# A causal depthwise convolution shared out anew between TensorE, VectorE, ScalarE and GpSimd, and another order of attention groups, in a two-layer encoder

## Chip, cores and metric

One core of one Trainium2 chip runs the whole kernel. The metric is the device time in microseconds of one execution, as the median of several runs.

## The reference

Input `x` is 1 x 256 x 1024 float32. Two layers, each a mixer and a feed-forward part, all with a residual sum. What bears on the change is the convolution module of layer 0 and the attention of layer 1:

```python
def conformer_conv_module(h, ...):
    u = h @ pw1_w + pw1_b
    a, gate = jnp.split(u, 2, axis=-1)
    u = a * jax.nn.sigmoid(gate)
    u = lax.conv_general_dilated(u, dw_w[:, None, :], window_strides=(1,),
        padding=[(CONV_WIDTH - 1, 0)], feature_group_count=D_MODEL, ...) + dw_b
    u = jax.nn.silu(layernorm(u, ln_g, ln_b))
    return u @ pw2_w + pw2_b
```

CONV_WIDTH is 31 and each of the 1024 channels has its own 31 taps. The layer norm is over the channels, so it needs all of them. Layer 0 then has a dense SwiGLU of width 2816. Keys and values for 4 heads are computed once from its result. Layer 1 is attention with 16 query heads of 64, four to a key head, over the own and the previous chunk of 64 tokens, with a learned sink per head and a relative-position bias:

```python
    scores = jnp.where(valid, scores + bias, -1e30)
    m = jnp.maximum(jnp.max(scores, axis=-1, keepdims=True), s)
    p = jnp.exp(scores - m)
    probs = p / (jnp.sum(p, axis=-1, keepdims=True) + jnp.exp(s - m))
    out = jnp.einsum("bckgqj,bcjkd->bcqkgd", probs, v_band)
    return out.reshape(B, S, N_HEADS * HEAD_DIM) @ w_o
```

A top-2-of-8 expert SwiGLU of width 3584 and a final norm end the kernel.

## The kernel before

The kernel is written engine by engine. Each engine has a fixed program, and semaphores join them; the order of work is the order in which it is written. PE is TensorE, DVE VectorE, ACT ScalarE, POOL GpSimd, SP the engine that issues most transfers.

Weights come in units of 1 MB through a ring of seven slots, issued by SP (L398, L453). From the dense stage on, a weight is used as the sum of two float32r parts: ACT copies a half unit (`high_parts`, L666), DVE subtracts the copy from the original (`low_parts`, L1410), and PE makes three passes (`three_passes`, L974). There is room for four halves of parts. A slot of the ring is loaded anew once DVE has split both of its halves (`split_done`). A `column_product` makes two 128-column pieces of a transposed product, a `row_product` adds one unit to the output in token rows.

**The convolution.** The 1024 channels are eight chunks of 128, a channel to a partition. The first pointwise product (L915) makes value and gate of two chunks at a time, on PE. ACT takes the sigmoid of a gate (L615), two buffers deep, and DVE multiplies (`glu`, L1349) into `upad`, which holds the chunk with 30 columns of zeros ahead. Then two engines share the 31 taps. DVE does chunks 0 to 4, one instruction of 128 x 256 a tap (`conv_tap`, L1356 for the first tap, L1359 for the others): each adds a shifted input times the tap's weights to the chunk, so a tap of a chunk waits for the one before it. Chunks go in pairs, (0,1), (2,3), and 4 alone; a further `glu` comes after every sixteen taps. PE does chunks 5 to 7: for a tap, one matmul (two records in the trace) of the shifted chunk with a diagonal matrix of the tap's weights, added up in a PSUM bank (L938). The diagonals are identity times the tap's column. ACT makes those with even numbers (L633), POOL those with odd ones (L517), into a ring `taps` of four that lies in `R1`, where the input of the first product is too; so they begin when that product is done, and each waits until the one four before it is used. ACT evicts a finished chunk with its bias (`conv_out`, L622). PE sums the chunks' columns with a matrix of 1/1024 (`add_to_mean`, L925): chunks 0 to 3, 5 and 6 ahead of the last four taps, 4 and 7 after them. DVE subtracts the mean (L1391), and the variance, the scaling and the second product (L961) follow.

**Attention.** Four groups, one for each key head. The unit of the query weights of a group is `U_Q + g`, that of the output weights `U_O + g`. For a group: `query_product` on PE, `queries` on ACT (copy with a scale), `scores` on PE (L1093) into two banks, `softmax_front` on DVE (sum with the bias, L1500; maximum, L1504; its negative with the sink, L1507), `exps` on ACT (L728), `softmax_sum` on DVE (L1514, L1515), the multiplication with the reciprocal on POOL (L559), `values` on PE (transposes L1102, ACT's copies `probs_T` L737, the product with V L1111) and `heads_out` on DVE (L1523, L1525), and `out_product` (L974). Groups of one parity share a pair of banks, a half of `prob` and a half of `bias`, so `scores(g)` waits for `heads_out(g - 2)`, and `softmax_front(g)` for the transposes of g - 2. POOL loads the bias of groups 0 and 1 ahead of the stage. Its program in the stage is, for g = 0 to 3: wait for the reciprocals, multiply, and for g = 0 and 1 issue the four transfers of the bias of group g + 2 (L544), wait for them and clear a corner (L549):

```python
                if g < 2:
                    pool.wait_ge(biased, 2 * g + 2)
                    load_bias(g + 2)
                    cut_bias(g + 2)
```

The experts follow with 336 units of weights, and take about two thirds of the time.

Of the kernel before, what the change touches and what calls it, by code (L numbers as in the profile page):

```python
# [57 lines left out]
DIAGS = 4  # L58
# [29 lines left out]
def expert_units():  # L88

    order = [("g", 0), ("u", 0)]  # L90
    for b in range(1, EB):
        order += [("g", b), ("u", b), ("d", b - 1)]
    order.append(("d", EB - 1))
    return [(kind, b, part) for kind, b in order for part in range(2)]


def trunk(nc, x, norm_mix_g, norm_ffn_g, conv_pw1_w, conv_pw1_b, conv_dw_w, conv_dw_b, conv_ln_g,
# [4 lines left out]
    with ctx:  # L102
# [62 lines left out]
        taps = R1[:, 1024:1024 + DIAGS * P].rearrange("p (b c) -> p b c", b=DIAGS)  # L165
# [85 lines left out]
        tap_pool = sem("tap_pool")  # L251
# [229 lines left out]
        def _(pool):  # L481
# [29 lines left out]
            product_done(pool, U_PW2 - 1)  # L511
            pool.wait_ge(cv_ready, 2)
            for m in range(1, PE_CHUNKS * CONV, 2):
                if m >= DIAGS:
                    pool.wait_ge(tap_used, m - DIAGS + 1)
                c, w = DVE_CHUNKS + m // CONV, m % CONV
                pool.tensor_scalar(taps[:, m % DIAGS, :], ident[:, :], dw[:, c, w:w + 1], 1.0, ALU.mult,  # L517
                                   ALU.mult).then_inc(tap_pool, 1)
# [58 lines left out]
        def _(sa):  # L577
# [39 lines left out]
            sa.wait_ge(cv_ready, 2)  # L617

            def conv_out(c):

                sa.wait_ge(tap_used, CONV * (c - DVE_CHUNKS + 1))
# [3 lines left out]
            conv_next = DVE_CHUNKS  # L625
            for m in range(0, PE_CHUNKS * CONV, 2):
                if m >= CONV * (conv_next - DVE_CHUNKS + 1) + DIAGS:
                    conv_out(conv_next)
                    conv_next += 1
                if m >= DIAGS:  # L630
                    sa.wait_ge(tap_used, m - DIAGS + 1)
                c, w = DVE_CHUNKS + m // CONV, m % CONV
                sa.mul(taps[:, m % DIAGS, :], ident[:, :], dw[:, c, w:w + 1]).then_inc(tap_act, 1)  # L633
            for c in range(conv_next, DC):
                conv_out(c)

# [109 lines left out]
            probs_T(0)  # L746
            exps(1)
            queries(3)
            high_parts(U_O + 1)
            probs_T(1)  # L750
            exps(2)
            high_parts(U_O + 2)
            probs_T(2)
            exps(3)
            high_parts(U_O + 3)
            probs_T(3)
# [101 lines left out]
        def _(pe):  # L858
# [59 lines left out]
            def add_to_mean(chunks):  # L918

                for c in chunks:  # L920
                    if c < DVE_CHUNKS:
# [7 lines left out]
            for m in range(PE_CHUNKS * CONV):  # L929

                c, w = DVE_CHUNKS + m // CONV, m % CONV
                if m % 2 == 0:
                    pe.wait_ge(tap_act, m // 2 + 1)
                else:
                    pe.wait_ge(tap_pool, m // 2 + 1)
                if w == 0:
                    pe.wait_ge(glu_ready, c + 1)
                mm = pe.matmul(PB[4 + m // CONV][:, 0:S], taps[:, m % DIAGS, :], upad[:, c, w:w + S],  # L938
                               start=(w == 0), stop=(w == CONV - 1))
                mm.then_inc(tap_used, 1)  # L940
                if m == PE_CHUNKS * CONV - 5:

                    add_to_mean([0, 1, 2, 3, 5, 6])
            add_to_mean([4, 7])
# [184 lines left out]
            scores(1)  # L1129
            values(0)  # L1130
            query_product(3)
            scores(2)
            values(1)
            out_product(0)
            scores(3)
            values(2)
            out_product(1)
# [150 lines left out]
        def _(ve):  # L1288
# [75 lines left out]
            pairs = [range(c, min(c + 2, DVE_CHUNKS)) for c in range(0, DVE_CHUNKS, 2)]  # L1364
            work = [(c, w) for pair in pairs for w in range(CONV) for c in pair]
# [4 lines left out]
            nxt = 2  # L1370
            for m, (c, w) in enumerate(work):
                if m % 16 == 15 and nxt < DC:
                    glu(nxt)
                    nxt += 1
                if w == 0:
                    ve.wait_ge(glu_ready, c + 1)
                else:
# [163 lines left out]
            softmax_sum(3)  # L1541
            low_parts(U_O + 3)
            heads_out(3)
# [231 lines left out]
```

## Time and profile before

| what | value |
|---|---|
| median of 3 runs | 1449.49 us (1448.54 to 1451.72) |
| the profiled execution | 1450.4 us, of which its span is 1448.7 us |
| PE, DVE, ACT, POOL busy | 98%, 81%, 68%, 4% of the span |
| mean granted clock of PE | 0.994 |

The profile is of one execution. Its page gives the busy time of each engine and the chain of work that ended last; the timelines give the instructions of an engine with start and duration in us, merged where they follow each other, and in brackets the idle time before them with what ended it. A busy PE means that a matmul is in flight, not that it is at its peak. Names are those of SBUF tensors: `R` stands for `R1`, `R2` and `R3`.

### The profile page before, as it was taken

The page shows a single profiled execution, that of the slowest core. Times are in us where ns is not written, and L with a number is a line of the kernel's source. Part 1 is how long each engine was busy: PE and PEld are TensorE (multiplying, and loading weights), DVE is VectorE, ACT ScalarE, POOL GpSimd, SP SyncE. Part 2 cuts the span into 40 slices and gives each one's busy share as a digit, 9 for nine tenths or more (in the row PEclk, how much of TensorE's full clock was granted, in tenths as well). Part 3 has the DMA queues.
Part 4 walks back from the last instruction along what each step waited for, and adds up shares of the span by engine and source line. Part 5 has one row for each costly group of instructions (what it writes and reads, how often), then busy time and mean ns, then how long its engine had stood idle before and what let it go on. Part 6 is the DMA issues. An engine that isn't in the chain of part 4 may idle for free.

```text
span 1448.7 us, 21504 instructions
## 1 busy us (share of the span) xinstructions
PE 1419.3 (98%) x7289; PEld 1193.2 (82%) x7289; DVE 1172.8 (81%) x1321; ACT 982.8 (68%) x1197; POOL 63.2 (4%) x108
## 2 busy tenths in 40 slices
PE   8999999999899999999999999999999999999997
PEld 8886899998878888888888888888888888888885
DVE  3793354456668998999999899899989989998996
ACT  2045343445646878877887877788888778877875
POOL 1060000002220000000000000000000000000000
PEclk9999999999999999999999999999999999999998
DMA  9500665555544999999899999999999999999991
GB/s 297 202 24 21 214 197 181 195 181 172 165 130 163 380 357 343 358 360 386 317 376 368 327 367 359 353 352 363 372 329 374 360 341 365 359 376 325 373 371 76
DMA packets 194064, 417.47 MB, mean 288 GB/s; under 512 B 6912, under 2 KB 43904, under 8 KB 194015
## 3 DMA queue, kind: packets, MB, share of 16 engines
q1 hardware_dynamic: 192510, 412.79, 79.6%
q0 software_dynamic: 1344, 3.98, 1.2%
q8 instruction: 31, 0.51, 0.1%
q14 instruction: 19, 0.15, 0.0%
q10 hardware_dynamic: 160, 0.04, 0.0%
HBM read 414.95 MB, written 1.84 MB: 288 GB/s over the span
## 4 chain that ended last, share of the span: by engine, by line
PE 93%; DVE 2%; ACT 2%; DMA 1%; POOL 1%; issue 1%; ACTq 0%; DVEq 0%; POOLq 0%
PE bank L974 77%; PE bank L915 4%; PE bank L938 3%; PE bank L961 2%; PE bank L1225 2%; PE bank L1176 1%; PE bank L1237 1%; DVE wl L1410 1%; PE bank L870 1%; ACT wh L666 1%; POOL prob L559 1%; DMA bias<-bias_scratch 0%; PE bank L882 0%; ACT prob L728 0%; DMA R<-in_conv_ln_b 0%
## 5 line engine op out<-in xcount | busy, mean ns | idle before, releaser
L1410 DVE TENSOR_TENSOR wl<-ring,wh 128x1024 fp32r<-128x1024 f32 x758 | 911.5, 1229 | 121.8 <-ACT wh L666 82.6
L666 ACT CAST wh<-ring 128x1024 fp32r<-128x1024 f32 x758 | 787.8, 1054 | 190.5 <-PE bank L974 190.4
L974 PE MATMUL bank<-wh,low 128*128 128x512 f32 (+1 forms) x1840 | 577.1, 393 | 3.5 <-DVE wl L1410 2.8
L974 PEld LDWEIGHTS bank<-wh,low 128*128 128x128 f32 x1840 | 339.9, 188 | 76.8 <-DVE wl L1410 8.9
L974 PE MATMUL bank<-wl,low 128*128 128x512 f32 x896 | 349.6, 390 | 0.0
L974 PE MATMUL bank<-wh,ath 128*128 128x512 f32 x528 | 206.3, 391 | 0.0
L974 PE MATMUL bank<-wh,atl 128*128 128x512 f32 x528 | 205.6, 389 | 0.0
L974 PE MATMUL bank<-wl,ath 128*128 128x512 f32 x528 | 205.5, 389 | 0.0
L974 PEld LDWEIGHTS bank<-wl,low 128*128 128x128 f32 x896 | 168.2, 188 | 36.1
L974 PEld LDWEIGHTS bank<-wl,ath 128*128 128x128 f32 x528 | 99.1, 188 | 20.8
L974 PEld LDWEIGHTS bank<-wh,ath 128*128 128x128 f32 x528 | 99.2, 188 | 20.2
L974 PEld LDWEIGHTS bank<-wh,atl 128*128 128x128 f32 x528 | 99.2, 188 | 19.8
L974 PE MATMUL bank<-high,wh 128*128 128x256 f32 x368 | 104.3, 283 | 0.7 <-DVE low L1421 0.7
L974 PE MATMUL bank<-high,wl 128*128 128x256 f32 x368 | 104.1, 283 | 0.0
L974 PE MATMUL bank<-low,wh 128*128 128x256 f32 x368 | 104.1, 283 | 0.0
L974 PEld LDWEIGHTS bank<-high,wh 128*128 128x128 f32 x368 | 70.6, 192 | 1.4 <-DVE low L1421 0.7
L974 PEld LDWEIGHTS bank<-high,wl 128*128 128x128 f32 x368 | 70.6, 192 | 0.4
L974 PEld LDWEIGHTS bank<-low,wh 128*128 128x128 f32 x368 | 70.6, 192 | 0.0
L1359 DVE SCALAR_TENSOR_TENSOR R<-R 128x256 f32<-128x256 f32 x150 | 64.6, 492 | 1.1
L494 POOL TENSOR_TENSOR rstd<-ms,mhalf 128x1 f32<-128x1 f32 x10 | 5.5, 552 | 1247.8 <-DVE ms L1299 1247.8
L915 PE MATMUL bank<-R,ring 128*128 128x256 f32 x256 | 55.5, 379 | 0.0
L915 PEld LDWEIGHTS bank<-R,ring 128*128 128x128 f32 x256 | 48.6, 190 | 6.9 <-issue 0.3
(214 smaller groups left out, 1070.1 us busy)
## 6 DMA issues: line engine op xcount, KB each, us to landing
ring<-in_moe_w_gate SPq DMA_DIRECT2D x112, 1024.0 KB, 6.1
ring<-in_moe_w_up SPq DMA_DIRECT2D x112, 1024.0 KB, 6.2
ring<-in_moe_w_down SPq DMA_DIRECT2D x112, 1024.0 KB, 6.4
ring<-in_conv_pw_w SPq DMA_DIRECT2D x12, 1024.0 KB, 10.9
ring<-in_ffd_w_gate SPq DMA_DIRECT2D x11, 1024.0 KB, 5.3
ring<-in_ffd_w_up SPq DMA_DIRECT2D x11, 1024.0 KB, 5.3
ring<-in_ffd_w_down SPq DMA_DIRECT2D x11, 1024.0 KB, 4.9
ring<-in_w_q SPq DMA_DIRECT2D x4, 1024.0 KB, 5.0
```

Source lines behind the costliest of these rows:

```text
L559: pool.tensor_tensor(prob[:, g % 2, t], prob[:, g % 2, t], spread(softm[:, g, 5, t, :].rearrange("p (h a) -> p h a", a=1), 2, BAND), ALU.m ...
L666: sa.copy(wh[:, place(n, h), :], ring_half(n, h)).then_inc(wh_ready, 1)
L870: pe.matmul(PB[bank][:, 0:P], ident[:, :], ident[:, :], start=True, stop=True)
L915: mm = pe.matmul(PB[2 * g + j % 2][:, c * S:(c + 1) * S], w[:, k, c * P:(c + 1) * P], hT[:, k, :], start=(k == 0), stop=(k == DC - 1))
L938: mm = pe.matmul(PB[4 + m // CONV][:, 0:S], taps[:, m % DIAGS, :], upad[:, c, w:w + S], start=(w == 0), stop=(w == CONV - 1))
L961: mm = pe.matmul(x_bank(t, half)[:, :], tokens(sq[:, k, :], t), w[:, k % 2, half * HALF:(half + 1) * HALF], start=(k == 0), stop=(k == DC ...
L974: mm = pe.matmul(out_bank, lhs, rhs, start=start and n == 0, stop=stop and n == 2, **kw)
L1176: mm = pe.matmul(PB[5 + half][:, :], pick[:, t, :], part[:, t, half * HALF:(half + 1) * HALF], start=(t == 0 and n == 0), stop=(t == 1 and ...
L1225: mm = pe.transpose(PB[2][:, j * P:(j + 1) * P], act[:, j * P:(j + 1) * P], ident[:, :])
L1237: mm = pe.matmul(PB[banks[half]][:, :], placeT[:, t * P:(t + 1) * P], part[:, half * HALF:(half + 1) * HALF], start=(n == 0), stop=(n == 1))
L1359: ins = ve.scalar_tensor_tensor(out=v, in0=upad[:, c, w:w + S], scalar=dw[:, c, w:w + 1], in1=v, op0=ALU.mult, op1=ALU.add)
L1410: ve.tensor_tensor(wl[:, place(n, h), :], ring_half(n, h), wh[:, place(n, h), :].bitcast(F32), ALU.subtract).then_inc(wl_ready, 1)
```

## The change

In the convolution, PE now does only 12 of the 31 taps of chunk 5, and all of chunks 6 and 7. ACT evicts the 12 taps' sum with the bias, and DVE adds the other 19 taps of chunk 5 to it. All diagonals are made by ACT, in a ring of sixteen which lies in `prob`; the first eight ahead of the third sigmoid, the next eight ahead of the fifth. POOL makes none. DVE's order of taps is written out: chunks 0 and 1; then 2 and 3, with the first 12 taps of chunk 4 among them; then the rest of 4 and 5 in turns. Its gate products come in pairs, ahead of taps 32, 68 and 98. PE adds chunks 0 to 3 and 6 to the mean ahead of the last four taps, and 4, 5 and 7 after them.

In attention the groups go in another order on PE, ACT and DVE, by the lists in the diff. POOL's program there stays, and so do all operations.

```diff
-DIAGS = 4
+DIAGS = 16
+SHARED_TAPS = 12
+def matrix_taps():
+    order = [(DVE_CHUNKS, w) for w in range(SHARED_TAPS)]
+    return order + [(c, w) for c in range(DVE_CHUNKS + 1, DC) for w in range(CONV)]
+def vector_taps():
+    order = [(c, w) for w in range(CONV) for c in (0, 1)]
+    for i in range(CONV):
+        order += [(2, i), (3, i)]
+        if 7 <= i < 7 + SHARED_TAPS:
+            order.append((4, i - 7))
+    return order + [(c, w) for w in range(SHARED_TAPS, CONV) for c in (4, DVE_CHUNKS)]
...
-        taps = R1[:, 1024:1024 + DIAGS * P].rearrange("p (b c) -> p b c", b=DIAGS)
+        taps = prob[:, :, :, :, :].rearrange("p b t h k -> p (b t h) k")
...
-            product_done(pool, U_PW2 - 1)
-            pool.wait_ge(cv_ready, 2)
-            for m in range(1, PE_CHUNKS * CONV, 2):
-                if m >= DIAGS:
-                    pool.wait_ge(tap_used, m - DIAGS + 1)
-                c, w = DVE_CHUNKS + m // CONV, m % CONV
-                pool.tensor_scalar(taps[:, m % DIAGS, :], ident[:, :], dw[:, c, w:w + 1], 1.0, ALU.mult,
-                                   ALU.mult).then_inc(tap_pool, 1)
...
+            def make_taps(some):
+                for m, (c, w) in some:
+                    if m >= DIAGS:
+                        sa.wait_ge(tap_used, m - DIAGS + 1)
+                    sa.mul(taps[:, m % DIAGS, :], ident[:, :], dw[:, c, w:w + 1]).then_inc(tap_act, 1)
             for c in range(DC):
+                if c == 2:
+                    sa.wait_ge(cv_ready, 2)
+                    make_taps(tap_list[0:8])
+                elif c == 4:
+                    make_taps(tap_list[8:DIAGS])
                 product_done(sa, U_PW1 + 2 * (c // 2) + 1)
...
+            made = DIAGS
+            for c in range(DVE_CHUNKS, DC - 1):
+                make_taps(tap_list[made:taps_to(c) + DIAGS])
+                made = taps_to(c) + DIAGS
                 conv_out(c)
+            make_taps(tap_list[made:])
+            conv_out(DC - 1)
...
# ACT, attention
-            probs_T(0)
             exps(1)
             queries(3)
+            probs_T(0)
             high_parts(U_O + 1)
             probs_T(1)
             exps(2)
+            exps(3)
+            probs_T(2)
             high_parts(U_O + 2)
-            probs_T(2)
-            exps(3)
+            probs_T(3)
             high_parts(U_O + 3)
-            probs_T(3)
...
# PE
-                if m % 2 == 0:
-                    pe.wait_ge(tap_act, m // 2 + 1)
-                else:
-                    pe.wait_ge(tap_pool, m // 2 + 1)
+                pe.wait_ge(tap_act, m + 1)
...
-                    add_to_mean([0, 1, 2, 3, 5, 6])
-            add_to_mean([4, 7])
+                    add_to_mean([0, 1, 2, 3, 6])
+            add_to_mean([4, 5, 7])
...
             scores(1)
+            query_product(3)
             values(0)
-            query_product(3)
+            values(1)
             scores(2)
-            values(1)
+            scores(3)
             out_product(0)
-            scores(3)
+            out_product(1)
             values(2)
-            out_product(1)
             values(3)
...
# DVE
+            glu_before = {32: (2, 3), 68: (4, 5), 98: (6, 7)}
+            for m, (c, w) in enumerate(vector_taps()):
+                for later in glu_before.get(m, ()):
+                    glu(later)
                 if w == 0:
                     ve.wait_ge(glu_ready, c + 1)
+                elif c == DVE_CHUNKS and w == SHARED_TAPS:
+                    ve.wait_ge(v_act, 1)
...
             softmax_sum(0)
+            softmax_front(1)
             low_parts(U_O)
-            softmax_front(1)
+            softmax_sum(1)
             heads_out(0)
-            softmax_sum(1)
+            heads_out(1)
             low_parts(U_O + 1)
             softmax_front(2)
-            heads_out(1)
+            softmax_front(3)
             softmax_sum(2)
+            softmax_sum(3)
+            heads_out(2)
             low_parts(U_O + 2)
-            softmax_front(3)
-            heads_out(2)
-            softmax_sum(3)
+            heads_out(3)
             low_parts(U_O + 3)
-            heads_out(3)
```

## Rows read from the trace of the kernel before

**Rows 1.** The page: shares of the chain that ended last, by engine

```profile
PE 93%; DVE 2%; ACT 2%; DMA 1%; POOL 1%; issue 1%; ACTq 0%; DVEq 0%; POOLq 0%
```

**Rows 2.** Timeline of PE, 20 to 162 us: start us, duration us, work

```profile
71.20 38.70 PE L938 MATMUL bank<-R 128*128 128x256 f32 x178 [1.22 <-ACT R L633]
109.75 2.75 PE L925 MATMUL bank<-R,ones 128*128 128x256 f32 x12
112.34 1.89 PE L938 MATMUL bank<-R 128*128 128x256 f32 x8
```

**Rows 3.** Timeline of DVE, the convolution: start us, duration us, idle before

```profile
42.91 0.48 DVE L1349 SCALAR_TENSOR_TENSOR R<-bank,cv,R 128x256 f32<-128x256 f32 x1 [6.94 <-ACT R L615]
43.31 6.42 DVE L1359 SCALAR_TENSOR_TENSOR R<-R 128x256 f32<-128x256 f32 x16
...
70.53 0.48 DVE L1349 SCALAR_TENSOR_TENSOR R<-bank,cv,R 128x256 f32<-128x256 f32 x1 [0.42 <-ACT R L615]
...
77.88 0.47 DVE L1349 SCALAR_TENSOR_TENSOR R<-bank,cv,R 128x256 f32<-128x256 f32 x1
78.27 12.77 DVE L1359 SCALAR_TENSOR_TENSOR R<-R 128x256 f32<-128x256 f32 x29
...
91.39 15.73 DVE L1359 SCALAR_TENSOR_TENSOR R<-R 128x256 f32<-128x256 f32 x30
115.53 0.82 DVE L1391 TENSOR_TENSOR R<-R,bank 128x640 f32<-128x640 f32 x1 [8.40 <-PE bank L925]
```

**Rows 4.** Timeline of ACT around the end of the first pointwise product

```profile
70.75 0.69 ACT L633 ACTIVATE R<-ident,R 128x128 f32<-128x128 f32 x2
```

**Rows 5.** PE groups from 374.60 to 421.25 us: busy us, mean ns, idle before

```profile
L1111 PE MATMUL bank<-R 128*64 128x128 f32 x64 | 5.9, 312 | 0.2
L1102 PE MATMUL bank<-ident,prob 128*128 128x128 f32 x32 | 5.2, 286 | 7.4 <-POOL prob L559 7.4
L1093 PE MATMUL bank<-R 64*64 64x128 f32 x128 | 4.6, 278 | 0.0
```

**Rows 6.** The chain that ended last, 340 to 470 us, in order of time

```profile
351.61 23.06 PE bank L974 x192
...
375.90 1.30 DVE prob L1500 x2
...
378.69 2.94 ACT prob L728 x15
...
382.51 3.04 POOL prob L559 x2
...
387.34 7.17 DMA bias<-bias_scratch
...
394.87 2.01 POOL prob L559 x2
...
421.25 11.11 PE bank L974 x48
```

**Rows 7.** DMA queues from 387 to 388 us (q0 POOL, q1 SP)

```profile
q0 software_dynamic: 66, 0.19, 79.9%
```

**Rows 8.** DMA queues from 389 to 390 us: packets, MB, share of 16 engines

```profile
q1 hardware_dynamic: 192, 0.39, 102.5%
q0 software_dynamic: 3, 0.00, 1.1%
```

**Rows 9.** Bias loads issued from 396 to 400 us, issue to landing

```profile
DMA to landing us min/median/max: 3.0/3.1/4.7
```

**Rows 10.** Timeline of SP: two ring loads issued, the first and the last start

```profile
381.15 5.88 SPq L453 DMA_DIRECT2D ring<-in_moe_w_up  x2
```

**Rows 11.** Timeline of DVE in attention, beside other work and beside POOL

```profile
378.77 2.35 DVE L1410 TENSOR_TENSOR wl<-ring,wh 128x1024 fp32r<-128x1024 f32 x2
...
383.43 3.21 DVE L1410 TENSOR_TENSOR wl<-ring,wh 128x1024 fp32r<-128x1024 f32 x2 [1.01 <-ACT wh L666]
```

**Rows 12.** Window of 5 us: PE, PEld, DVE, ACT, POOL busy, granted clock, DMA

```profile
397.00:402.00 5.00, 5.00 (x28) 3.71 (x29) 4.90 (x8) 1.01 (x3) 2.28 (x4) 0.66 0.68 181
```

More of the change, by code:

```diff
@@ L250, in trunk @@
         tap_act = sem("tap_act")
-        tap_pool = sem("tap_pool")
         tap_used = sem("tap_used")
@@ L609, in _ @@
             norm_out(0, hT, CV_MIX0)
-            for c in range(DC):
+            tap_list = list(enumerate(matrix_taps()))
+            def make_taps(some):
[3 more added lines that the diff above has]
+                    sa.mul(taps[:, m % DIAGS, :], ident[:, :], dw[:, c, w:w + 1]).then_inc(tap_act, 1)
+            for c in range(DC):
+                if c == 2:
[3 more added lines that the diff above has]
+                    make_taps(tap_list[8:DIAGS])
                 product_done(sa, U_PW1 + 2 * (c // 2) + 1)
@@ L616, in _, with taps_to @@
                               bias=cv[:, CV_PW1B + DC + c:CV_PW1B + DC + c + 1]).then_inc(sig_ready, 1)
-            sa.wait_ge(cv_ready, 2)
+            def taps_to(c):
+                return SHARED_TAPS + CONV * (c - DVE_CHUNKS)
             def conv_out(c):
-                sa.wait_ge(tap_used, CONV * (c - DVE_CHUNKS + 1))
+                sa.wait_ge(tap_used, taps_to(c))
                 sa.activation(v_chunk(c), PB[4 + c - DVE_CHUNKS][:, 0:S], ACT.Identity,
                               bias=cv[:, CV_DWB + c:CV_DWB + c + 1]).then_inc(v_act, 1)
[L625 to L634, printed above, removed]
+            made = DIAGS
+            for c in range(DVE_CHUNKS, DC - 1):
+                make_taps(tap_list[made:taps_to(c) + DIAGS])
+                made = taps_to(c) + DIAGS
                 conv_out(c)
+            make_taps(tap_list[made:])
+            conv_out(DC - 1)
             sa.activation(warm[:, 0:1], eps[:, 0:1], ACT.Sqrt).then_inc(tables, 1)
@@ L920, in add_to_mean @@
                 for c in chunks:
-                    if c < DVE_CHUNKS:
+                    if c <= DVE_CHUNKS:
                         pe.wait_ge(v_dve, c + 1)
@@ L927, in add_to_mean @@
                     mm.then_inc(mean_done, 1)
-            for m in range(PE_CHUNKS * CONV):
-                c, w = DVE_CHUNKS + m // CONV, m % CONV
-                if m % 2 == 0:
-                    pe.wait_ge(tap_act, m // 2 + 1)
-                else:
-                    pe.wait_ge(tap_pool, m // 2 + 1)
+            for m, (c, w) in enumerate(matrix_taps()):
+                pe.wait_ge(tap_act, m + 1)
                 if w == 0:
                     pe.wait_ge(glu_ready, c + 1)
-                mm = pe.matmul(PB[4 + m // CONV][:, 0:S], taps[:, m % DIAGS, :], upad[:, c, w:w + S],
-                               start=(w == 0), stop=(w == CONV - 1))
+                last_tap = SHARED_TAPS - 1 if c == DVE_CHUNKS else CONV - 1
+                mm = pe.matmul(PB[4 + c - DVE_CHUNKS][:, 0:S], taps[:, m % DIAGS, :], upad[:, c, w:w + S],
+                               start=(w == 0), stop=(w == last_tap))
                 mm.then_inc(tap_used, 1)
-                if m == PE_CHUNKS * CONV - 5:
-                    add_to_mean([0, 1, 2, 3, 5, 6])
-            add_to_mean([4, 7])
+                if m == len(matrix_taps()) - 5:
+                    add_to_mean([0, 1, 2, 3, 6])
+            add_to_mean([4, 5, 7])
             keep_busy(1, 10)
@@ L1361, in conv_tap @@
                 return ins
-            pairs = [range(c, min(c + 2, DVE_CHUNKS)) for c in range(0, DVE_CHUNKS, 2)]
-            work = [(c, w) for pair in pairs for w in range(CONV) for c in pair]
             tap_at = {}
@@ L1369, in _ @@
             ve.wait_ge(glu_ready, 2)
[L1370 to L1374, printed above, removed]
+            glu_before = {32: (2, 3), 68: (4, 5), 98: (6, 7)}
+            for m, (c, w) in enumerate(vector_taps()):
+                for later in glu_before.get(m, ()):
+                    glu(later)
                 if w == 0:
                     ve.wait_ge(glu_ready, c + 1)
+                elif c == DVE_CHUNKS and w == SHARED_TAPS:
+                    ve.wait_ge(v_act, 1)
                 else:
```

## The prediction

> **What bounds the kernel now.** I read four things in this order. First the page's chain that ended last: 93% of it is PE [rows 1], so a change pays only where it shortens PE's work or a gap of PE. Then PE's timeline through the convolution, to see which it is there: after the first product PE waits 1.22 us for the first diagonal, then runs 89 taps (178 records, two to a tap) in 38.70 us without a gap, which is 0.435 us a tap, then six matmuls of the mean, then the last four taps [rows 2]. The ring of four diagonals therefore costs nothing today except those 1.22 us. PE's own pace is the bound. Third, DVE's timeline over the same stretch: its last tap ends at 107.12 us and it then idles 8.40 us until the mean is there [rows 3]. DVE has room that PE lacks. Fourth, attention, where the groups of PE from 374.60 to 421.25 us show 7.4 us of idle time before the transposes of the probabilities, all put down to POOL, and 0.2 us before the products with V [rows 5]. The chain in order of time says what POOL was doing in the longest case: not multiplying, but waiting 7.17 us for a bias load [rows 6].
>
> **The convolution, part by part.** *Taps leave PE.* 93 become 12 + 62 = 74. That removes 19 x 0.435 = 8.3 us from PE [rows 2].
>
> *The first diagonals are made early.* ACT makes sixteen while the first product runs, so PE goes on at 69.98 (71.20 less the idle 1.22) [rows 2]. That is 1.2 us. The diagonals now live in the tile that attention uses later, so they don't collide with the input of the product.
>
> *All diagonals by ACT.* Two in 0.69 us with nothing to wait for [rows 4], so about 0.35 us each against PE's 0.435. With sixteen slots each is made some 15 taps before its use, and the wait on a used slot ends at PE's own pace. 74 x 0.35 = 26 us of ACT, of which sixteen lie ahead of 70 us; it hides behind PE's taps. I cost it at nothing. Without that cover each diagonal would add a hand-over between the engines to PE's path, the 1.22 us above at worst.
>
> *DVE gets 19 taps.* 155 become 174. In the undisturbed stretch sixteen taps and what follows them start 6.33 us apart (43.31 to 49.64, the next gate product, if the last 0.09 us of 6.42 is the pipeline's tail), so 0.396 us a tap. Beside POOL's diagonals 29 taps take 12.77 us, 0.44 each, while the gate product in the midst of it, whose one input is in PSUM, stays at 0.47 against 0.48 us. The fifth chunk ran alone, each tap waiting for the last: 30 in 15.73 us, 0.524 each [rows 3]. The new order never runs a chunk alone and POOL makes no diagonals, so 0.396 holds for all. It also does 32 taps ahead of the third gate product, which fills the 6.94 us of idle time before 42.91 [rows 3]. The walk: first tap at 30.1 us (the third gate product's 42.91, less the 6.94 idle, less 15 taps); 32 taps to 42.8; two gate products from 42.91 to 43.7; 36 taps to 58.0; two more to 58.7; 30 taps to 70.6, when the seventh gate's sigmoid is just there (70.53 before) [rows 3]; two more to 71.4; 76 taps to 101.5.
>
> *The end of the stage.* PE: 70 taps from 69.98 to 100.4; five matmuls of the mean at 0.43 (six from 109.91 to 112.50 before) to 102.6; four taps to 104.3; the mean of chunks 4 and 5, which covers ACT's eviction of the last chunk, to 105.2; and 0.7 for the last matmul with its tail, 105.9. DVE is done at 101.5, so chunks 4 and 5 don't wait. DVE starts to subtract the mean at about 106.0 instead of 115.53 [rows 3]. **Gain 9.6 us**: 8.3 + 1.2 + 0.4 (a matmul less ahead of the last taps) - 0.3 (one more behind them). What follows, to the start of attention, is released by PE's progress and moves as a whole.
>
> **Attention, part by part.** No work is added or removed; PE does the fourth query product before the values of group 0 and pairs the groups. Everything is the same until PE ends the scores of group 1 at about 382.6: the fourth product of the stage ends at 374.67 (351.61 + 23.06), and scores, a query product and scores follow [rows 6]. Durations: a query product 23.06 / 4 = 5.8 us; four transposes 5.2 / 8 = 0.65; values with V 5.9 / 4 = 1.5; scores 1.15 [rows 5, 6]. A softmax front on DVE takes 2.8 us (375.90 to 378.69), and the exponentials 3.3 (the row's 15 of 16 records, and two short ones) [rows 6].
>
> *DVE and ACT.* The front of group 1 now comes ahead of the split of the first output unit: 382.7 to 385.6. Exponentials to 388.9. PE's query product ends at 388.5, its copy at 389.4. The values of group 0 go to PE at 388.5 and end at 391.3, with some 0.3 us lost to the copies.
>
> *POOL.* This is what decides. It multiplies group 0 from 382.51. That took 3.04 us beside DVE's split and 2.01 without a DVE operation ahead of it [rows 6]; DVE's pair of splits took 3.21 beside it against 2.35 [rows 11]. DVE now does the front there, whose input is in PSUM with one in SBUF, so I take 2.0 to 3.0 us. Then it issues four bias loads (the last one 4.8 us after the multiplication's start at 382.51, or 3.8), waits for them, clears their corner in 0.3 us, and only then multiplies group 1. The load that cost 7.17 us was issued at 387.34; SP's ring load at 386.66 (381.15 + 5.88 less the issue itself, 0.37) [rows 6, 10]. While the bias ran alone its queue had 79.9% of the engines; once the ring was flowing it had 1.1% against 102.5% [rows 7, 8]. The four issued from 396 us, ahead of a ring load, landed in 3.0 to 4.7 us [rows 9]. In the new order the split that releases the ring load comes after the front, 385.6 to 388.0 or later, so the bias load gets 1.5 to 2 us ahead. It lands at 389.4 to 392.0 instead of 394.51, and group 1 is multiplied by 391 to 394 instead of 396.87.
>
> The Trainium skill ("DMA: Bandwidth & Descriptors", section on queues, rings and completion order) says that each DMA engine takes a packet in turn from every queue that has work. By that rule the bias queue would have kept about half the engines beside the ring, the ring load would not explain 7.17 us, and moving it would win next to nothing; the sum would then be the first rival's. The 1.1% in [rows 8] speaks against an even share, in this microsecond at least.
>
> *PE from there.* Values of group 1 end at 394.7 to 396.5, against 399.4 before (396.88, then the second transposes 0.65, a copy and the last products). Scores 2 (1.15), 0.4 of waiting for the heads of group 1, scores 3 (1.15), two output products (11.11 / 2 = 5.6 each) [rows 6], values 2 in 2.7, values 3 in 3.1 (ACT splits a unit between their copies). Sum 19.7, so the last two output products start at 414.4 to 416.2 instead of 421.25. Softmax of groups 2 and 3 is ready some 2 us before PE asks; the bias load of group 3 too. **Gain 5.0 to 6.9 us.** The clock is open: from 397 to 402 us the granted clock averages 0.66 of 2.4 GHz, so most of it was at the lower level of 1.2 GHz, 5 x 0.34 = 1.7 us lost, after the waits for the transposes [rows 12]. I have counted it as regained. It may stay, or strike elsewhere, so I take 6.0.
>
> **The sum.** The profiled execution took 1450.4 us, its span 1448.7. 1450.4 - 9.6 - 6.0 = 1434.8. The median of the runs is 0.9 below the profiled one (1449.49), so **1433.9 us**. Bounds of the unknowns: 1.0 more in attention and 1 more elsewhere from the shifted clock, 1431.8; the rivals below up to 1440.
>
> **Rivals.**
> *The bias load is late all the same.* If the landing is bound by the latency of the load or by the ring load's packets however late, group 1 is multiplied at 396.9 as before. Values 1 end at 399.4, and the walk's 19.7 us lead to 419.1: 2.1 us of gain, less half of the 1.7 of slow clock, 1.3. For it: the loads at one time took 3.0 and at another 7.17 with only a guess at the cause. Against it: [rows 7 to 9]. Result 1438.6.
>
> *DVE paces the convolution a little.* If ACT, not POOL, is what stretches taps to 0.44, then the 76 taps after 71.4 end at 104.9 and the mean follows 0.8 us later than I say; were all 174 so slow, DVE ends at 109.2 and 5 us go. Results 1434.7 to 1438.9. Against it: the gate product at 77.88 was not stretched, and ACT worked beside DVE's splits at 378.77 without harm [rows 3, 11].
>
> *DVE becomes the bound outright.* Its end is at 32.6 + 174p. At p = 0.524, the chained pace of the lone chunk [rows 3], it ends at 123.8, the mean at 125.5, 10 us later than before, and with attention's 6.0 the kernel takes 1453.4. It costs more than it gives from p = 0.50 on. Against it: pairs have run at 0.396 for 62 taps, and every new stretch has two or three chunks.
>
> *It doesn't do what it says*: PE's taps stretch so that 74 take as long as 93 (0.55 us), through a diagonal that comes late. Then 0.5 to 1 us of change and 6 of attention: about 1442. ACT's 0.35 speaks against it [rows 4].
>
> **How the numbers follow.** Forecast 0.62 (1432 to 1436.5), late bias 0.22, a little pacing 0.09, no gain in the convolution 0.03, DVE the bound 0.03, others 0.01. To leave out no more than 2 in 10 the range takes the first three: 1431.5 to 1440.0. A change of 0.2% is 2.9 us, about what a measurement of this kernel can tell from none. Faster 0.96, same 0.01, slower 0.03.
>
> **What the profile would show.** 148 records of taps from about 70.0 us in 32 us with the mean's matmuls between them; DVE's last tap near 101.5; the subtraction at 106.0; no POOL work there. In attention, shifted by 9.6: the bias load's wait 3 to 4.7 us, idle time before the transposes under 2 us instead of 7.4, 41 us from the third query product to the last two output products instead of 46.65. I am wrong if DVE's taps leave 0.396, or the bias load still takes 7 us.

## The result, and the profile after

The changed kernel takes 1430.84 us in the median of 4 runs (1430.4 to 1435.97), against 1449.55 us of the kernel before. The ratio is 0.9874, with a 95% interval from 0.9862 to 0.9885. I had said 1433.9 us and a range of 1431.5 to 1440.0: the direction is right, the gain of 18.7 us is larger than the 15.6 that I forecast, and the time lies 0.7 us below the range. One execution of one experiment below (`e9_nine_and_split`) took 2873.69 us, for a reason that no run shows, and its ratio leaves it out.

Four stretches can be cut out of both traces. The columns are the start of the subtraction of the mean (DVE's first operation after the convolution), the start of the 192 records that open the stage of keys, values and queries, the end of the last output product of attention, and the end of the span.

| | subtraction | start of K, V, Q | end of attention | span |
|---|---|---|---|---|
| before | 115.53 | 351.61 | 432.36 | 1448.7 |
| after | 104.98 | 341.06 | 413.68 | 1428.9 |
| stretch before | 115.53 | 236.08 | 80.75 | 1016.34 |
| stretch after | 104.98 | 236.08 | 72.62 | 1015.22 |

So the convolution gave 10.55 us, 0.45 of which had come before PE began its taps (the first product ends at 69.54 instead of 69.99 us; the other profiles of this study, with the same code up to there, end it between 69.5 and 70.8). The dense stage moved as a whole, to a hundredth. Attention gave 8.13 us, and the experts and the end 1.12.

PE's timeline after, through the convolution. Its rows answer to [rows 2].

```profile
59.66 9.88 PE L936 MATMUL bank<-R,ring 128*128 128x256 f32 x45
69.37 30.39 PE L956 MATMUL bank<-R,prob 128*128 128x256 f32 x140
99.60 2.32 PE L946 MATMUL bank<-R,ones 128*128 128x256 f32 x10
101.76 1.89 PE L956 MATMUL bank<-R,prob 128*128 128x256 f32 x8
103.49 1.46 PE L946 MATMUL bank<-R,ones 128*128 128x256 f32 x6
```

PE goes from the product to the taps without a gap, where it waited 1.22 us. 140 records, 70 taps, take 30.39 us with their tail, 0.43 a tap as before. The six records of the last mean follow the last four taps at once, so chunks 4 and 5 hide ACT's eviction. DVE's timeline, which answers to [rows 3]:

```profile
42.45 0.88 DVE L1367 SCALAR_TENSOR_TENSOR R<-bank,cv,R 128x256 f32<-128x256 f32 x2 [0.21 <-ACT R L637]
43.24 11.96 DVE L1377 SCALAR_TENSOR_TENSOR R<-R 128x256 f32<-128x256 f32 x30
...
70.08 0.87 DVE L1367 SCALAR_TENSOR_TENSOR R<-bank,cv,R 128x256 f32<-128x256 f32 x2
70.88 30.16 DVE L1377 SCALAR_TENSOR_TENSOR R<-R 128x256 f32<-128x256 f32 x76
104.98 0.82 DVE L1409 TENSOR_TENSOR R<-R,bank 128x640 f32<-128x640 f32 x1 [3.94 <-PE bank L946]
```

The idle time ahead of the third gate product has gone from 6.94 to 0.21 us. The 76 taps after the last gate product take 30.16 us, 0.396 each, though three chunks or two take turns and one of them is in another tile. DVE still idles 3.94 us ahead of the mean: PE sets the end. ACT's timeline answers to [rows 4]:

```profile
28.86 2.44 ACT L625 ACTIVATE prob<-ident,R 128x128 f32<-128x128 f32 x8
...
70.30 4.86 ACT L625 ACTIVATE prob<-ident,R 128x128 f32<-128x128 f32 x12
75.06 0.46 ACT L647 ACTIVATE R<-bank,cv 128x256 f32<-128x256 f32 x1
75.42 13.13 ACT L625 ACTIVATE prob<-ident,R 128x128 f32<-128x128 f32 x31
```

Eight diagonals take 2.44 us, 0.3 each, in ACT's idle time beside the first product (the next eight, from 42.67 us, the same). From 75.42 us on 31 take 13.13 us, 0.42 each. That is not ACT's own pace but PE's, since each waits for a slot.

In attention, the groups of PE from the first scores to the last two output products (38.52 us, 46.65 before) answer to [rows 5], the chain to [rows 6], and the bias load to [rows 9]. First the groups (busy us, mean ns, idle before):

```profile
L1111 PE MATMUL bank<-R 64*64 64x128 f32 x128 | 4.6, 277 | 0.5 <-DVE low L1543 0.5
L1129 PE MATMUL bank<-R 128*64 128x128 f32 x64 | 4.6, 279 | 1.8 <-ACT R L758 1.7
L1120 PE MATMUL bank<-ident,prob 128*128 128x128 f32 x32 | 4.5, 277 | 0.3 <-POOL prob L567 0.3
```

(L1120 are the transposes, L1129 the products with V, L1111 the scores.) The wait before the transposes is 0.3 us where it was 7.4. A new 1.7 us stands before the products with V, put down to ACT's copies. The chain, in order of time:

```profile
341.06 23.06 PE bank L992 x192
...
371.96 2.04 POOL prob L567 x2
...
375.79 3.31 DMA bias<-bias_scratch
...
379.46 2.01 POOL prob L567 x2
...
386.28 11.11 PE bank L992 x48
...
402.57 11.11 PE bank L992 x48
```

The first multiplication takes 2.04 us where it took 3.04, and the last of the four loads of the bias of group 2 takes 3.31 where it took 7.17. It still lands last: the reciprocals of group 1 are ready at 378.75, and their multiplication begins at 379.46. Issue to landing of the four loads:

```profile
DMA to landing us min/median/max: 3.2/3.3/3.3
```

The granted clock answers to [rows 12]. It is 1.00 in the first output products (387 to 392 us here) and in all of the stretch of attention. The low stretch that is left before the experts lies in the routing, and the kernel before had one there too:

```profile
387.00:392.00 5.00, 5.00 (x23) 4.13 (x22) 4.85 (x9) 2.06 (x11) 0.00 (x0) 1.00 0.63 210
419.00:424.00 5.00, 5.00 (x32) 5.00 (x32) 4.03 (x18) 1.96 (x3) 0.00 (x0) 0.66 0.00 2
```

### The profile page after: what moved, and what is told of

Read it like the earlier page. It is cut to its first block, busy times and chain, and to the rows that moved or that the text cites. A ratio compares the mean times of both kernels' runs of the same rounds, so it can differ in the third digit from the quotient of the medians.

```text
span 1428.9 us, 21427 instructions
## 1 busy us (share of the span) xinstructions
PE 1406.5 (98%) x7251; PEld 1185.9 (83%) x7251; DVE 1170.0 (82%) x1340; ACT 990.4 (69%) x1224; POOL 35.8 (3%) x62
## 4 chain that ended last, share of the span: by engine, by line
PE 94%; DVE 2%; ACT 2%; issue 1%; POOL 1%; DMA 0%; DVEq 0%; POOLq 0%; ACTq 0%
PE bank L992 78%; PE bank L936 4%; PE bank L956 2%; PE bank L979 2%; PE bank L1243 2%; PE bank L891 1%; PE bank L1194 1%; PE bank L1255 1%; DVE wl L1428 1%; ACT wh L687 1%; PE bank L903 0%; ACT low L812 0%; POOL prob L567 0%; PE bank L1205 0%; PE bank L967 0%
## 5 line engine op out<-in xcount | busy, mean ns | idle before, releaser
L1679 DVE TENSOR_TENSOR atl<-bank,ath 128x512 fp32r<-128x512 f32 x56 | 38.3, 684 | 10.5 <-ACT ath L827 10.5
```

What stands on the lines that cost most here:

```text
L1679: ve.tensor_tensor(atl[:, :, :], PB[2][:, :].rearrange("p (j s) -> p j s", j=4), ath[:, :, :].bitcast(F32), ALU.subtract).then_inc(atl_rea ...
```

## Experiments

Each was timed in five rounds beside the kernel before on the same chip.

**The two halves.** `e1_conv_only` is the changed kernel with the lists of attention set back, `e2_attention_only` the kernel before with the new lists. Of the lists, PE's in `e2_attention_only` for one:

```diff
             scores(1)
+            query_product(3)
             values(0)
-            query_product(3)
+            values(1)
             scores(2)
-            values(1)
+            scores(3)
             out_product(0)
-            scores(3)
+            out_product(1)
             values(2)
-            out_product(1)
             values(3)
```

> The convolution's half of the change alone, attention in the order of before. If the two halves are independent, the gain is that of the profile's convolution stretch, 10.1 to 10.6 us (the subtraction of the mean at 104.98 instead of 115.53 us), about 1439 us, and the stretch of attention takes its old 46.65 us with a bias load that waits some 7 us and a granted clock under 1 for a few us. If instead the clock's low stretch moved away because the phase of the stages shifted (and not because the waits went), attention is some 1.7 us shorter here too, about 1437.5 us.

> The other half alone, the convolution as before. If the halves are independent, the gain is 8.1 us, about 1441.4 us: the profile after has 38.5 us in place of 46.65. If part of the 8.1 us came from the shifted phase of the clock, it gains 6.4 to 7. If the late bias load was chance, it gains 2 to 4.

Measured: 1440.65 us against 1450.1, ratio 0.9934 (0.9920 to 0.9947), and 1442.59 us, ratio 0.9950 (0.9937 to 0.9964). The product of the two is 0.9884, at the upper end of the interval of the whole change. In the profiles `e1_conv_only` has the stretch of attention at 80.29 us and `e2_attention_only` at 72.54, and from the end of the first product to the subtraction 35.45 and 45.54. The halves are independent. In `e1_conv_only`, where the phase has moved by 10 us, attention has two low stretches of the clock instead of one; in `e2_attention_only` it has none. Two windows of the first, then one of the second:

```profile
374.50:378.50 4.00, 2.96 (x20) 2.33 (x20) 3.96 (x5) 0.89 (x2) 3.40 (x5) 0.57 0.60 172
398.00:403.00 5.00, 4.88 (x27) 3.73 (x28) 4.86 (x8) 1.75 (x7) 0.07 (x1) 0.66 0.53 173
```

```profile
374.60:413.50 38.90, 36.18 (x374) 31.40 (x372) 25.12 (x42) 28.30 (x89) 13.54 (x18) 1.00 0.42 136
```

(Columns: PE, PEld, DVE, ACT and POOL busy, granted clock, DMA share, GB/s.) So of these two profiles the old lists have low stretches in attention and the new ones have none. The order of work does not decide where they fall: counted from the start of the keys, values and queries, the clock falls after 46 us in the kernel before, and after 33 and 57 us in `e1_conv_only`, in the same order of work. The first of these falls ahead of the bias load, whose last part is issued at 377.27 us. What a half gives in the median, 9.45 and 7.5 us, is 0.6 and 0.7 us less than its stretch shows.

**Is it the ring load that delays the bias load?** In the kernel before, SP holds one ring load back until the bias of group 2 has landed, and nothing else changes:

```diff
                     split_done(sp, n - RING, 1, i)
+                    if u == 3 and isinstance(i, int):
+                        sp.wait_ge(bias_in[2], 64)
```

> The kernel before in the old order, but SP issues the ring load that follows the split of the first output unit only when the bias of group 2 has landed. Theory 1, the ring load starves the bias load: the bias lands some 3 us after its last issue instead of 7.2, POOL multiplies group 1 at its reciprocals' time or shortly after, PE's wait before the transposes of group 1 shrinks from 1.8 us to near nothing, and the kernel gains 1 to 2 us, since other waits of the old order stay (their sum was 7.4 us). Theory 2, the even turn of queues or a latency of the bias load itself: the load still takes over 5 us, and the time stays within 0.5 us of before.

Measured: 1449.74 us against 1450.1, ratio 0.9991 (0.9980 to 1.0002), so no change that can be told. But the load itself answers. Four bias loads, issued at 385.7 to 387.5 us as before the change:

```profile
DMA to landing us min/median/max: 2.8/2.9/3.0
```

Before, the same four had 3.0, 4.9 and 7.2 us. Theory 1 stands for the load: with the ring load out of the way it is on time, so it was the ring load that delayed it. The even share of the queues falls too, though not by as much as the microsecond in [rows 8] says. In the kernel before, from 388 to 392 us:

```profile
q1 hardware_dynamic: 493, 1.00, 81.4%
q0 software_dynamic: 73, 0.19, 18.1%
```

The bias queue moved one packet for seven of the ring's, most of them at the end (36.7% of the engines against 70.1% from 391 to 392 us). In the stretch the held load bought 1.70 us (80.75 to 79.05), and the granted clock of the stretch went from 0.98 to 1.00. PE's waits hardly moved:

```profile
PE bank L1104 <- POOL prob L561: 6.6, 7, 1.4
PE bank L1113 <- ACT R L739: 0.7, 1, 0.7
```

6.6 and 0.7 us, against 7.4 and 0.2. So most of the 1.70 us is, by subtraction, the clock's. POOL was no longer held up by the load, but the reciprocals of group 1 came only just before its multiplication (393.22 and 393.30 us), and the other groups wait as ever. In the kernel before the same reciprocals end at 393.05:

```profile
392.85 0.20 DVE L1515 RECIPROCAL small<-small 128x8 f32<-128x8 f32 x1
```

The multiplication began at 394.87 [rows 6]. Of the 7.17 us that the chain gives to the load, 1.8 held POOL up; through the others it would have waited for the reciprocals in any case.

**The first front and split on DVE apart from the rest of the lists.** In the changed kernel, the split of the first output unit goes back ahead of the front of group 1; in the kernel before, the front goes ahead of the split. All other entries of the lists, DVE's too, stay as they are in either kernel.

```diff
# e4_split_first, in the changed kernel
+            low_parts(U_O)
             softmax_front(1)
-            low_parts(U_O)
             softmax_sum(1)
# e11_front_first_old_order, in the kernel before
+            softmax_front(1)
             low_parts(U_O)
-            softmax_front(1)
             heads_out(0)
```

> The changed kernel, but DVE splits the first output unit ahead of the softmax front of group 1, as before the change. Theory 1 (starved bias load): POOL's multiplication takes 3.0 us again, the ring load meets the bias load, which takes about 7 us, and values of group 1 wait on PE for some 3 to 4 us: 1434 to 1435 us. Theory 2 (the order of PE's products alone makes the gain): within 1 us of the changed kernel, about 1431 us.

> The kernel before in all but one place: DVE does the softmax front of group 1 ahead of the split of the first output unit. With the kernel before (neither), the changed kernel (both) and the one with the split first (new order alone) this fills a table of two by two for the stretch of attention, so far 80.75 (neither), 77.96 (new order alone) and 72.62 us (both). Theory, the bias load is starved by the ring load that the split releases: the multiplication takes 2.0 us, the bias lands some 3.3 us after its last issue, as when the ring load was held back, and the low stretch of the clock in attention goes; since group 1's softmax is also ready earlier, the stretch takes 76.5 to 78.5 us. If the two parts simply added it would be 80.75 - (77.96 - 72.62) = 75.4 us. Rival: in the old order the order on DVE is worth no more than the held ring load, 79.05 us, as PE has other work until the load lands.

Measured: `e4_split_first` 1436.36 us, ratio 0.9903 (0.9888 to 0.9918); `e11_front_first_old_order` 1448.27 us against 1449.65, ratio 0.9996 (0.9987 to 1.0005). The chains of the two, the first fence `e4_split_first`:

```profile
342.32 23.07 PE bank L992 x192
...
379.84 0.18 DVE small L1525
...
380.04 1.69 ACT prob L749 x9
...
383.80 0.48 ACT R L758
...
384.42 2.00 PE bank L1129 x16
386.42 1.90 PE bank L1120 x8
...
409.17 11.11 PE bank L992 x48
```

```profile
351.95 23.06 PE bank L974 x192
...
382.85 2.05 POOL prob L559 x2
...
418.86 11.11 PE bank L974 x48
```

With the end of the last output products less the start of the 192 records, the stretch of attention is:

| | the other entries old | the other entries new |
|---|---|---|
| split first on DVE | 80.75 | 77.96 |
| front first on DVE | 78.02 | 72.62 |

Each alone gives 2.7 to 2.8 us, both 8.1: 2.6 us come only together. In `e4_split_first` the multiplication takes 3.05 us and the load up to 6.5:

```profile
DMA to landing us min/median/max: 2.9/5.0/6.5
```

```profile
PE bank L1129 <- ACT R L758: 5.4, 3, 4.4
```

Yet, against my expectation, the one wait of 4.4 us is not the load's. It stands before the products with V of group 0, at 384.42 us, and the chain above does not pass through the load at all. ACT's new list has the exponentials of group 1 ahead of the copies of group 0. With the split first, DVE ends the front of group 1 at 380.01 us instead of 375.00, which is 3.75 later when the 1.26 us of phase are taken off, and only then can ACT go on; the products with V of group 0 start 3.75 us later too (384.42 against 379.41). Behind this wait the late load is hidden: POOL multiplies group 1 from 384.89 us, and PE comes to its transposes at 386.35 without waiting. The other 1.6 of the 5.3 us between this kernel and the changed one come after that. PE's clock is low from 383 to 389.6 us, and its 40 records from 384.42 to 390.12 us take 5.8 us, which unbroken and at full clock take 3.3 (1.11, 1.09 and 1.11 in the changed kernel). So what ties the two parts together is ACT's list, which pays only if DVE's front comes early. No run has the new lists with a late load and nothing else, so what the load alone would cost them is open.

For `e11_front_first_old_order` the stretch says 2.7 us and the median 1.4, and the interval of its ratio includes no change. Its last load landed after 4.0 us. The stretches are of one execution each.

**What the ring's depth is worth.**

```diff
-DIAGS = 16
+DIAGS = 4
...
-                    make_taps(tap_list[0:8])
+                    make_taps(tap_list[0:DIAGS])
                 elif c == 4:
-                    make_taps(tap_list[8:DIAGS])
+                    pass
```

> The changed kernel with a ring of four diagonals in place of sixteen, all still by ACT and the first four still made during the first product. Theory: PE's taps run at their own 0.435 us and ACT's round trip (0.46 us of hand-over and 0.40 of work, 0.86) fits into a ring of four (1.74 us), so the depth is worth nothing and only the early start counts: within 0.3 us of the changed kernel in the convolution, its end-of-product to subtraction stretch 35.4 us. Rival: the depth is what lets one engine make all diagonals; then PE's taps stretch towards 0.5 us and the stretch becomes 40 us.

Measured: 1431.4 us against 1450.16, ratio 0.9862 (0.9843 to 0.9881). The end of PE's product, its taps, and DVE's subtraction:

```profile
59.69 10.31 PE L936 MATMUL bank<-R,ring 128*128 128x256 f32 x47
69.83 30.39 PE L956 MATMUL bank<-R,prob 128*128 128x256 f32 x140
```

```profile
105.45 0.82 DVE L1409 TENSOR_TENSOR R<-R,bank 128x640 f32<-128x640 f32 x1 [3.94 <-PE bank L946]
```

From the end of the product (70.00) to the subtraction 35.45 us, as in the changed kernel (69.54 to 104.98, 35.44). 140 records in 30.39 us, the same. Twelve of the sixteen slots are worth nothing; one engine and four slots suffice.

**How many taps to move.** `SHARED_TAPS = 9` and `SHARED_TAPS = 6` in the changed kernel:

> The changed kernel with nine taps of chunk 5 on PE in place of twelve, so three more on DVE. DVE idled 3.94 us ahead of the subtraction, three taps cost it 1.2 us and PE gives up 3 x 0.435 = 1.3 us. Theory that PE still sets the end: subtraction 1.3 us earlier, about 1429.5 us. Rival, DVE sets the end by now: no gain or a loss.

> Six taps of chunk 5 on PE. DVE's last tap comes 2.4 us later than in the changed kernel, at about 103.4 us, PE's last tap 2.6 us earlier, at 101.0. Then DVE ends last and the mean of chunks 4 and 5 waits for it: subtraction at about 104.8, 0.2 us before that of the changed kernel and 1.1 after that of the version with nine.

Measured: 1430.32 us, ratio 0.9862 (0.9841 to 0.9883), and 1432.35 us, ratio 0.9869 (0.9849 to 0.9889). The subtraction with nine, then the last mean and the subtraction with six:

```profile
104.25 0.82 DVE L1409 TENSOR_TENSOR R<-R,bank 128x640 f32<-128x640 f32 x1 [1.46 <-PE bank L946]
```

```profile
103.08 1.56 PE L946 MATMUL bank<-R,ones 128*128 128x256 f32 x6 [2.02 <-DVE R L1377]
```

```profile
104.68 0.82 DVE L1409 TENSOR_TENSOR R<-R,bank 128x640 f32<-128x640 f32 x1 [1.26 <-PE bank L946]
```

With nine it is 34.15 us from the end of the product (70.10) to the subtraction, 1.3 less than with twelve. With six PE waits 2.02 us for DVE's last tap, and it is 35.15 us (from 69.53). The bound passes from PE to DVE between the two, as expected. The medians don't separate nine from twelve: 1430.32 us where I expected about 1429.5.

**What stretched DVE's taps before.** POOL makes 37 diagonals beside the changed kernel's taps, into a tile that is free there; nobody reads them.

```diff
+            pool.wait_ge(cv_ready, 2)
+            for m in range(1, 74, 2):
+                pool.wait_ge(tap_used, m)
...
+                pool.tensor_scalar(bias[:, m // 2 % 2, m // 4 % 2, m // 8 % 4, :], ident[:, :], dw[:, 7, 0:1], 1.0,
+                                   ALU.mult, ALU.mult).then_inc(pool_junk, 1)
```

> The changed kernel, and beside the taps POOL makes 37 diagonals that nobody uses, of the same form and at the same pace as before the change. Theory 1, POOL's work stretched DVE's taps from 0.396 to 0.44 us: the 76 taps from 70.88 us on take some 33.4 us instead of 30.2 and end at about 104.2, so the mean comes about 0.8 us later than the changed kernel's. Theory 2, it was ACT's diagonals beside them: no change, 30.2 us.

```profile
71.36 32.65 DVE L1386 SCALAR_TENSOR_TENSOR R<-R 128x256 f32<-128x256 f32 x76
105.48 0.82 DVE L1418 TENSOR_TENSOR R<-R,bank 128x640 f32<-128x640 f32 x1 [1.46 <-PE bank L955]
```

76 taps take 32.65 us instead of 30.16, 0.43 each, with nothing but POOL's work added: it was POOL. But I expected 33.4 and a mean 0.8 us later, and the mean came at its old place, 35.45 us after the end of the product (70.03): DVE's last tap at 104.01 still lies ahead of PE's at 104.14. The median was 1430.23 us, ratio 0.9862 (0.9843 to 0.9881). With twelve taps POOL's absence from the diagonals is worth nothing in the end, it only makes room.

**A better version?** ACT copies the high parts of the third output unit ahead of the copies of group 2, alone and with nine taps.

```diff
             exps(3)
+            high_parts(U_O + 2)
             probs_T(2)
-            high_parts(U_O + 2)
             probs_T(3)
```

> The changed kernel, but ACT copies the high parts of the third output unit ahead of the copies of group 2's transposes instead of between those of groups 2 and 3. In the chain of the changed kernel the copy of the high parts (1.9 us) stands between the values of groups 2 and 3 on PE's path. Theory that this is the last avoidable wait in attention: the copies of group 2 come some 0.4 us later, those of group 3 at once, and the stretch of attention falls from 72.6 to about 71.5 us. Rival: the wait moves ahead of the copies of group 2, no change.

> Both improvements together on top of the changed kernel: nine shared taps, and the high parts of the third output unit ahead of the copies. If both hold and add, the stretch to the subtraction is 1.3 us and that of attention about 1 us shorter than in the changed kernel, and the median 1428 to 1429 us; the place of the low stretches of the clock may blur 1 to 2 us of it.

Measured: 1431.29 us, ratio 0.9867 (0.9851 to 0.9884), and 1430.38 us, ratio 0.9860 (0.9841 to 0.9880), where I expected 1428 to 1429. The stretch of attention is 72.82 us in the first and 72.80 in the second: no gain. The chain of the first shows where it went:

```profile
396.92 1.89 ACT wh L687 x2
...
402.00 1.14 DVE wl L1428
...
403.28 11.13 PE bank L992 x48
```

The same 1.89 us of copying now stands ahead of the copies of group 2, and behind it PE waits for DVE's split of that unit, which ends at 403.14. The wait moved, as the rival had it. So nine taps is all that was found beyond the change: 1.3 us in the convolution's stretch, not resolved in the medians.

## Why the prediction was right and wrong

*PE bounds the convolution, 19 taps less, the early start.* Right. Forecast 9.6 us, measured 10.1 from the end of the product to the subtraction (45.54 to 35.44). Two tails were counted as time: the first tap starts 0.17 us before the product's modelled end, and the last three matmuls of the mean take 1.3 us after the last tap where I had 1.6. The other 0.45 of the 10.55 us lies ahead of the taps and is not the change's.

*ACT alone, and the ring.* Right that it costs nothing, but not for the reason given. I took the sixteen slots as the cover without which each diagonal would add a hand-over to PE's path. The ring of four takes the same 35.45 us, so four slots are cover enough.

*DVE at 0.396 a tap.* Right, to the last digit: forecast end 101.5, measured 101.04 with the product's end 0.45 earlier. POOL, not ACT, was the cause of 0.44, so the second rival falls; the third, a pace of 0.524, falls by the 0.396 itself.

*The bias load.* Right in that the ring load delays it: with that load held back it took 3.0 instead of 7.2 us, and in the new order, which issues it later, 3.3. The first rival had it late all the same and falls. With it falls what I drew from the rule of the Trainium skill ("DMA: Bandwidth & Descriptors", section "Queues, rings and completion order") that an engine takes packets in turn from the queues that have work: about half the engines for the bias queue. It got 18.1% against 81.4% from 388 to 392 us, and no run shows how the turns went. But "This is what decides" is not shown. Of the 7.17 us only 1.8 held POOL up in the kernel before, since the reciprocals of group 1 were not there sooner. Holding the ring load back alone moved PE's waits by 0.3 us. And with the split first in the new lists the loss went through ACT's exponentials and not through the load. The walk did have the front of group 1 earlier as well, but gave it no weight of its own.

*The step that failed: the sum of attention, "Gain 5.0 to 6.9 us", of which I took 6.0.* It measured 8.1. Two terms make the 2.1. First, I took back 0.9 us for a low stretch of the clock that "may stay, or strike elsewhere". It was gone after the change, and in every profile in which the bias load was on time; it stayed in the three in which it was late (before, `e1_conv_only` and `e4_split_first`). That is no cause shown: in `e1_conv_only` the first of two low stretches comes ahead of the load, and in `e4_split_first` it follows another wait. Second, I took the lengths of values and transposes from [rows 5], 5.9 and 5.2 us for the stretch. The same work takes 4.6 and 4.5 us after. Two things were in the rows of before. Some records ran at the lower clock, which I had counted as a loss of its own in [rows 12] and left inside the durations too: in the two runs with PE's old list and a clock of 1.00 (`e3_ring_waits_for_bias`, `e11_front_first_old_order`) the products with V take 5.1 us, in the three with a low stretch (before, `e1_conv_only`, `e4_split_first`) 5.9 to 6.3. And where a wait stands between two bursts, each burst ends with its own tail, which the busy time holds and an unbroken run does not: the transposes take 5.0 to 5.2 us in those two runs, though at full clock, and 4.5 in the new order.

What it did to the walk: PE has the values of groups 0 and 1 done and starts the output products at 386.28 us, 396.83 in the old count (10.55 added), where the early end of the walk has 397.4. Values 2 and 3 take 5.2 us (386.28 + 11.11 = 397.39 to 402.57), not 5.8. In these the two errors stand side by side: I had 5.6 us of work and 0.2 of waiting, and the trace has 4.3 of work and 1.1 of waiting for ACT's copies, which overlap by 0.2. Together that is the 1.2 us above the walk's upper end of 6.9.

*The rest.* I had it unchanged, and it was 1.1 us shorter. That is within what it varies by without a change to it. From the end of attention to the end of the span the profiles of thirteen kernels, whose code is the same there, have between 1014.35 (`e1_conv_only`) and 1018.42 us (`e4_split_first`). The first has no low stretch of the clock in the routing, the second one of 10 us. The last windows of before and after differ in PE's clock, 0.88 against 0.93 (the second is the changed kernel's):

```profile
1407.36:1448.36 41.00, 31.77 (x143) 25.20 (x141) 30.16 (x35) 23.09 (x29) 1.10 (x2) 0.88 0.30 117
```

```profile
1388.68:1428.90 40.22, 30.06 (x139) 24.05 (x137) 29.12 (x33) 22.49 (x28) 1.09 (x2) 0.93 0.29 111
```

A range that ends 2.4 us below its middle was too narrow for this alone. Why the low stretches fall where they do is not settled.

*The whole sum.* The profiled execution was forecast at 1434.8 us and took 1430.62. The 4.2 us are 2.1 of attention, 0.5 of the convolution, 0.45 ahead of it and 1.1 of the rest. Against that, I took 0.9 us off since the median lay below the profiled execution before; after the change it lies 0.2 above. That term was chance, and so it is by luck that the time missed the range by 0.7 us and not by more.

## What to carry to other kernels

Take durations from an unbroken stretch whose granted clock is 1.00, or the price of work that will run fast holds slow clock and the tails of broken bursts, as here 0.3 us in each group. A small transfer can be delayed by a large one that another engine's step releases: look at what that step would release, and let the small load go first. The length of a wait in the chain is not its price: ask when the other inputs were ready (here 1.8 of 7.17 us counted). Where one engine's list puts a step of the next group ahead of one of this group, it pays only if the engine that feeds it does likewise. A two-by-two table tells that the orders hang together, and only the chain tells through which engine.

## What was not expected of the hardware

The four bias loads of 128 KB each for group 2 landed in 2.8 to 3.4 us ahead of the ring load (up to 4.0 in `e11_front_first_old_order`) and in up to 7.2 beside a ring load of 1 MB on another queue (6.7 and 6.5 us in two other runs). From 388 to 392 us the smaller queue had 18.1% of the engines, and 1.1% in the worst microsecond [rows 8]. And the same end of the kernel took up to 4 us more or less from profile to profile, with PE's clock at the lower level for none to 10 us in the routing and for 3 to 10 us at the end.
